# Input loads in another order, values' low parts earlier on VectorE, and more idle products near the end of a two-layer diffusion step

## What is computed

```python
h = rms_norm(x, norm1_g) * (1 + scale1) + shift1        # scale, shift from silu(cond) @ w_ada + b_ada
aq, ak, av, bq, bk, bv, cq, ckv, ckr, du = split(h @ w_in)
# A: differential attention on rotated aq, ak; B: neighbourhood attention with a learned bias;
# C: attention whose q, k, v come from rms_norm(cq) @ c_wuq and rms_norm(ckv) @ c_wukv,
#    half of each head rotated; D: a convolution branch
x = x + gate1 * ((sigmoid(h @ w_gate + b_gate) * branches).sum() @ w_out)
x = x + gate2 * hier_moe(rms_norm(x, norm2_g) * (1 + scale2) + shift2)
y = rms_norm(x, final_norm_g)                            # after both layers
```

## Time and profile before

| | us |
|---|---|
| median of 3 runs (range) | 1729.57 (1729.35 to 1730.38) |
| the profiled execution | 1730.84 |
| its span, first to last instruction | 1729.0 |
| PE busy in the span | 1619.5 (94%) |
| DVE / ACT / POOL busy | 1174.8 / 888.5 / 479.4 |
| mean granted TensorE clock | 0.984 of full speed |

### The profile page before, as it was taken

One profiled execution on the slowest core, in us unless ns is written; L12 is line 12 of the kernel. 1 busy time (PEld: TensorE's weight loads), 2 busy tenths in 40 slices (PEclk: granted clock), 3 DMA queues, 4 the chain that ended last, 5 costly groups with the idle time before them and its releaser, 6 DMA issues.

```text
span 1729.0 us, 33919 instructions
## 1 busy us (share of the span) xinstructions
PE 1619.5 (94%) x13291; PEld 1097.4 (63%) x13291; DVE 1174.8 (68%) x1877; ACT 888.5 (51%) x1477; POOL 479.4 (28%) x460
## 2 busy tenths in 40 slices
PE   6999999999999996999889999999999999889996
PEld 4678776777776565544467887677777755645544
DVE  4594475777735856899666937577774494779974
ACT  4322555666643133787652236466665411348864
POOL 1332263212232211223053326322122321022214
PEclk9999999999999998999999999999999999989998
DMA  9674545532146555999994443322223476579975
GB/s 324 205 257 149 178 141 193 202 117 77 58 135 245 178 210 219 333 404 406 344 324 125 147 138 100 91 97 79 78 77 109 140 244 220 207 267 405 406 301 203
DMA packets 191628, 351.49 MB, mean 203 GB/s; under 512 B 15796, under 2 KB 99315, under 8 KB 191219
## 3 DMA queue, kind: packets, MB, share of 16 engines
q1 hardware_dynamic: 183141, 320.92, 52.6%
q0 software_dynamic: 7776, 28.32, 4.4%
q10 hardware_dynamic: 557, 0.14, 0.0%
HBM read 288.32 MB, written 61.01 MB: 202 GB/s over the span
## 4 chain that ended last, share of the span: by engine, by line
PE 67%; DVE 13%; DMA 7%; ACT 5%; issue 4%; DVEq 1%; SPq 1%; POOL 1%; ACTq 0%; POOLq 0%
PE PS L447 40%; PE PS L454 12%; PE PS L1243 3%; PE PS L1227 3%; DMA y_rows<-scratch 3%; PE PS L1000 2%; DMA arena<-in_moe_w 2%; DVE arena L2665 1%; PE PS L960 1%; PE PS L977 1%; DMA hpart<-y_rows,wulo 1%; SPq L815 1%; PE PS L1376 1%; DMA wf<-in_w_out 1%; DVE arena L2864 1%
## 5 line engine op out<-in xcount | busy, mean ns | idle before, releaser
L1978 POOL TENSOR_TENSOR wlo<-wf,whi 128x256 f16<-128x256 f32 (+2 forms) x300 | 301.7, 1039 | 813.1 <-ACT whi L1600 773.7
L447 PE MATMUL PS<-hpart,whi 128*128 128x320 f16 x2048 | 423.0, 300 | 6.3 <-ACT arena L1686 6.0
L447 PE MATMUL PS<-hpart,wlo 128*128 128x320 f16 x1024 | 306.5, 299 | 0.0
L447 PEld LDWEIGHTS PS<-hpart,whi 128*128 128x128 f16 x2048 | 190.0, 98 | 93.2 <-issue 24.5
L447 PE MATMUL PS<-whi,hpart 128*128 128x256 f16 (+1 forms) x1280 | 202.9, 268 | 0.0
L447 PE MATMUL PS<-wlo,hpart 128*128 128x256 f16 (+1 forms) x640 | 169.3, 268 | 0.0
L447 PE MATMUL PS<-arena 128*128 128x64 f16 (+1 forms) x1944 | 165.6, 236 | 2.3 <-DVE arena L2864 2.3
L2471 DVE TENSOR_REDUCE stat<-PS 128x1 f32<-128x640 f32 (+1 forms) x160 | 110.7, 713 | 76.4 <-PE PS L1227 73.8
L454 PE MATMUL PS<-hpart,whi 128*128 128x128 f16 (+1 forms) x768 | 137.5, 302 | 8.1 <-DVE hpart L2143 3.9
L1686 ACT ACTIVATE arena<-PS,pcol 128x320 f32<-128x320 f32 x128 | 67.4, 527 | 148.7 <-PE PS L447 141.4
L2299 DVE SCALAR_TENSOR_TENSOR scratch<-scratch,cw 128x655 f32<-128x655 f32 x120 | 138.6, 1197 | 4.8 <-issue 0.4
(11 more groups left out here) (375 smaller groups left out, 2939.5 us busy)
## 6 DMA issues: line engine op xcount, KB each, us to landing
arena<-in_moe_w SPq DMA_DIRECT2D x56, 1024.0 KB, 13.5
arena<-in_w_ada SPq DMA_DIRECT2D x48, 1024.0 KB, 8.5
wf<-in_w_gate SPq DMA_DIRECT2D x32, 1024.0 KB, 6.1
wf<-in_moe_w SPq DMA_DIRECT2D x28, 1024.0 KB, 13.1
g_rows<-arena SPq DMA_DIRECT2D x128, 160.0 KB, 1.8
wf<-in_w_in SPq DMA_DIRECT2D x18, 1024.0 KB, 7.6
y_rows<-scratch SPq DMA_DIRECT2D x34, 512.0 KB, 12.2
arena<-g_rows SPq DMA_DIRECT2D x24, 640.0 KB, 5.0
```

The lines of the kernel that those rows point to most:

```text
L447: ins = pe.matmul(out, st, mv, start=first and n == 0, stop=last and n == 2)
L1978: ins = pool.tensor_tensor(lo[:, a:b], wf[j][:, a:b], hi[:, a:b], ALU.subtract)
```

## The change

Four edits:

1. SP issues `ident` and the five x tiles first, and the six small loads behind them; `ident` is counted with the first pair of x tiles. PE no longer waits for `consts_in` before its first transpose, but before L945. DVE waits for the first pair and for the six small loads where it waited for all seven.
2. `values_low` moves, within steps 1, 2 and 5 of DVE's loop, from the step's end to the place behind `normed(n + 1)`.
3. `idle(10)` becomes `idle(24)` in layer 1; layer 0 keeps 10.
4. `idle(6)` in the last loop becomes `idle(5)`.

```diff
         def _(sp):
-            for dst, src in ((ident[:, :], t["k_ident"]),
-                             (crow[0:KC, :], t["c_ctx"].rearrange("(k p) -> k p", p=P)),
+            sp.dma_start(ident[:, :], t["k_ident"]).then_inc(xs_in[0].sem, 16)
+            for tile in range(TILES):
+                src = t["x_prompt"][0] if tile == 0 else t["x_sample"][0, P * (tile - 1):P * tile, :]
+                sp.dma_start(xtok[:, tile, :], src).then_inc(xs_in[tile // 2].sem, 16)
+            for dst, src in ((crow[0:KC, :], t["c_ctx"].rearrange("(k p) -> k p", p=P)),
...
                 sp.dma_start(dst, src).then_inc(consts_in.sem, 16)
-            for tile in range(TILES):
-                src = t["x_prompt"][0] if tile == 0 else t["x_sample"][0, P * (tile - 1):P * tile, :]
-                sp.dma_start(xtok[:, tile, :], src).then_inc(xs_in[tile // 2].sem, 16)
...
-            pe.wait_ge(*consts_in(0, 7 * 16))
             for tile in range(TILES):
-                pe.wait_ge(*xs_in[tile // 2](0, 32 if tile < 4 else 16))
+                pe.wait_ge(*xs_in[tile // 2](0, (48, 32, 16)[tile // 2]))
...
             pe.wait_ge(*x_moved(0, 1))
+            pe.wait_ge(*consts_in(0, 6 * 16))
             pe.transpose(PS[:, 1, 0:3 * KC], crow[:, :], ident[0:3 * KC, 0:3 * KC]).then_inc(xt_done.sem, 1)
...
-                idle(10)
+                idle(10 if ahead else 24)
...
-                                idle(6)
+                                idle(5)
...
-            dve.wait_ge(*consts_in(0, 7 * 16))
+            dve.wait_ge(*xs_in[0](0, 48))
+            dve.wait_ge(*consts_in(0, 6 * 16))
             dve.drain()
...
                     elif n + 1 == TILES:
                         dve.nop().then_inc(cn_ready.sem, 1)
+                    if n in (1, 2, TILES):
+                        values_low(min(n - 1, 2))
                     if n:
                         dve.wait_ge(*c_hi(l, n))
...
                         else:
                             dve.nop().then_inc(qkc_ready.sem, 1)
-                    if n in (1, 2, TILES):
-                        values_low(min(n - 1, 2))
```

More of the change, by code:

```diff
@@ L1517, in square_rows @@
             def square_rows(tile):
-                act.wait_ge(*xs_in[tile // 2](0, 32 if tile < 4 else 16))
+                act.wait_ge(*xs_in[tile // 2](0, (48, 32, 16)[tile // 2]))
                 act.activation(sqr[:, tile, :], xtok[:, tile, :], ACT.Square, accum_out=stat[:, 2, tile:tile + 1]
```

## The result

The changed kernel takes 1736.91 us (median of 6 runs, 1735.61 to 1738.97), the kernel before 1729.97 beside it (6 runs, 1726.88 to 1731.32). The profiled execution of after took 1735.78 us with a span of 1733.9. That is 4.9 more than the span of before, while the medians are 7 apart: single executions lie up to 3 us off their median, and the profiled one of after is the second lowest of its six.

The account below looks back on a forecast made before the run. PE, busy for 94% of the span, was taken to bound the kernel. Start +0.7, values_low +0.6 and end 0 gave 1729.57 + 1.3 = 1730.9 us, forecast as no change, with a range of 1726.5 to 1735.2.

Parts of the forecast that it names:

- PE bounds the kernel: Whole kernel: PE works for 94% of the span, so whatever moves PE's instruction stream moves the end.
- x tiles first, the small loads late: Start: x tiles come some 2.1 us earlier; the small loads stand behind 2.6 MB, `k_band` in at 14.5 (13.9 to 16.0).
- the early of the two cases: Start: first pair of x tiles in near 6.2 us if one engine held up all tiles, otherwise at 9.4.
- the 31 rows: Start, `k_band`'s load: by the skill's rule on the outer dimension, 31 rows go through one DMA engine.
- `crow` at 18.0: Start: `crow` turned at 18.0 instead of 18.57, a gain of 0.6 us (1.2 gain to 0.9 loss).
- The clock, 1.3 us: Start: PE's half-clock stretch after its wait costs 1.3 us, half of the largest price of 2.5.
- the long one: Start: PE stands 4.8 us until 18.0 after its x-tile transposes; the short case was 1.6 us.
- the bound of 2.5: Start: largest price of PE's slow stretch, 2.5 us for the 5 us of the first start.
- values_low, +0.15 a place: Preparation: DVE and POOL turns sum about the same; +0.15 us at each of four places for PE's transposes, +0.6.
- turns fall worse: Preparation, rival: one more POOL instruction of 1.27 us ahead of each L2398, +5.1, total 1735.4; chance 0.16.
- The end, 0: End: PE keeps its speed for L1477, DVE's addition moves up 1.73 us, but DVE waits for ACT; gain 0.
- The sum: Whole kernel: 0.7 + 0.6 + 0 us, so +1.3 on the median 1729.57, giving 1730.9: no change.

## Why the prediction was wrong

- **PE bounds the kernel**: right. It is busy for 94% of both spans, and what moved PE's stream moved the end.
- **x tiles first, the small loads late**: right. The first transpose stands at 6.28, the early of the two cases (6.2). The Trainium skill (DMA: Bandwidth & Descriptors, on why a DMA increments its semaphore by 16) gave this case; the landing agrees, though no run splits the 31 rows to show that one engine is the cause. `k_band` was forecast at 14.5 within 13.9 to 16.0 and came at 15.3.
- **`crow` at 18.0**: 0.65 too early, by the later landing; +0.1 instead of -0.6. In the five traces with the new order and DVE's old sequence the cast of `k_band` starts at 15.3 to 16.6 and L945 at 19.2 on average, against 18.8 in the four with the old order: +0.4, so this term missed by 1.0. That DVE's wait for `k_band` is the gate was shown by the kernel in which DVE copies first.
- **The clock, 1.3 us**: the step that failed most. The wait was the long one, 5.44, for which the text itself had "should cost", and the term was still cut to half of the bound. Idle products and the first `w_ada` units ran at half clock until near 24.5, and L1024 stands at 27.15 where it was 24.37, 2.8 later, of which `crow` has 0.1: the price is 2.7, the bound of 2.5 slightly exceeded. A further 1.6 by 57 us comes from a second slow stretch (L1000 2.47 at 44.04), which before has later, behind 53.03; so it is partly given back. In all the start costs +3.1 in the first trace, 4.1 on average of the five traces (4.4 against the mean of the four in the old order), and 4.7 in the times; the forecast had +0.7 with a top of 3.4. That the clock makes the price is shown by the kernels with idle products in the wait: `crow` is followed by 1.00 in all three.
- **values_low, +0.15 a place**: the second step that failed, "so the sum is about the same". At the first place DVE's chain grew from 12.31 to 12.47, +0.16; the forecast's 0.15 matches by luck, as it stood for PE's transposes and not for DVE's chain. At the second it grew from 11.58 to 12.40, +0.82. There L2361 meets POOL's L2004 (L2002 at the first place) and takes 1.53 instead of 0.53 (+1.00), L2381 2.40 instead of 1.97 (+0.43) behind POOL's late L1978, and only 0.47 comes back at L2358 and 0.22 at L2340 and L2341. Counting turns at one place was not enough: what POOL loses in step 1 goes by way of PE's gate products and ACT's L1600 into POOL's start in step 2. +0.98 per layer, +2.0 in all instead of +0.6; shown by every trace with this part and by none without. The times have 2.2, good to 1.3. The rival "turns fall worse" had the direction, not its 5.1. That single instructions change by 0.7 (L2340 at the first place) and 1.0 (L2361) with their order fits the Trainium skill (SBUF — State Buffer, SBUF: two separate sides) better than shared bandwidth would; the runs don't isolate it.
- **The end, 0**: right in the number (0.6 in the times, good to 1.3). Its first step, that PE keeps its speed for L1477, held in one of the five traces with 24 idle products (1.09); in the others L1477 took 1.75 to 1.97. In that one trace DVE's wait for ACT took the gain as forecast (2.05; forecast 2.4).
- **The sum**: +1.3 forecast. The start's 4.7 and values_low's 2.2 in the times give 6.9, beside 6.9 and 6.2 measured for the whole; each of the two is good to 1.3 only, so the close fit is in part luck. The range ended at 1735.2, since the text took both terms at their upper ends for unlikely together; one was above its bound.

What stays open: why `k_band` takes so long, and why a slow stretch comes at one of several places. Traces differ in it where their programs don't, and so no version could be given a clock gain with certainty. The stretch behind step 3 of layer 0 shows the same: from that L2398 to the next it is 8.5 to 8.8 us in ten of all fourteen traces and 7.1 in four, with values_low early and late, a difference of up to 1.7 us that no part of the change explains.

## What to carry to other kernels

When a load is moved behind others, look for the engine that waits for it *in order ahead of other work*: DVE waited for `k_band` and so kept back a copy that had no need of it, which made a head start of 5 us into a wait of 5 us. A long wait of PE (5.4 us and more: all five traces) should be charged with the full price of the half-clock stretch behind it, and where an edit shifts such stretches, the price is read at a landmark beyond all of them. Where two engines take turns, follow the chain through every place of a loop, and through the other engines between two places, since what one place delays sets the start of the next; and for effects of a tenth of a per cent, time all combinations of the parts and read a landmark in each trace.

## What the hardware showed unexpectedly

- The small loads were slow on both queues: `k_band` issued by 7.0 us from SP's queue was in at 15.3, and issued by 3.1 us from ScalarE's queue at 18.6, and ScalarE's issues held that engine until 14.64.
- The clock fell behind a wait of 0.5 us, after short products (L1024's of 56 columns and L977's of 2), in two kernels (at 30 and at 25 us), and did not fall at that place in a third whose program is the same up to there.
- DVE's and POOL's turns repeat to 0.05 us: step 1 to step 3 takes 23.9 us in every trace with values_low late in the step, and 24.9 in every trace with it early, in both layers, whatever the start did.
